# Eight of forty expert steps select their token rows with TensorE instead of gathering them, and one token tile's shared-expert products move later

## The chip, the cores and the metric

The kernel runs on one core of one Trainium2 chip. The metric is the device time of one execution in microseconds (us); the kernel before takes 987.73 us, the median of three runs. All data are f32 unless the text says otherwise.

## What is computed

One decoder layer for 512 tokens of 1024 channels. The first half (a pooling mixer and a windowed attention, gated and projected) is not touched by the change. The second half, cut to what matters:

```python
h2 = rmsnorm(x, g_ffn).reshape(T, D)             # T = 512, D = 1024
idx, wts = route(h2, w_router, router_bias)      # 8 of 64 experts a token, limited to groups
moe = routed_experts(h2, idx, wts, w_exp_gate, w_exp_up, w_exp_down) \
    + swiglu(h2, w_sh_gate, w_sh_up, w_sh_down)  # the shared expert
x = x + moe.reshape(B, S, D)
ple_gate = sigmoid(rmsnorm(x, g_ple) @ w_ple_gate)
x = x + ple_gate * rmsnorm(p @ w_ple_proj, g_ple_post)

def swiglu(x, wg, wu, wd):                       # inner width 256, also for each expert
    return (silu(x @ wg) * (x @ wu)) @ wd
```

Every expert has 3 MB of weights (gate, up and down of 1 MB each), so the 64 of them are the bulk of what the kernel reads.

## The kernel before, in words

**Tiles and order.** The 512 tokens are four tiles of 128. The residual x lies in `xrow` (128 x 4 x 1024) through the whole second half. The residual's rows, normed and multiplied by g_ffn (h2), are also stored in DRAM (`h2_rows`). After routing, the experts are put in an order by their number of tokens: the first four are fixed, the rest descends. They are worked off four at a time (a group). Each expert of the first eight groups has 96 places, each of the last eight has 64. A step is 128 places, so a big group has three steps and a small one two: steps 0 to 23 are big, steps 24 (`SMALL_AT`) to 39 small, and a small step holds exactly two experts.

**One step r** is spread over the engines:

- POOL (`move`, L830) gathers the step's rows of h2 from DRAM by an indirect DMA (L821) into one of three buffers `hg` (in `rows`), three steps ahead, as soon as `rows_T(r)` has read the buffer; and it scatters the weighted results of step r to an accumulator in DRAM (L826). Both take their row numbers from a staging tile (L814, L818), and a small operation (a ticket, L809) goes ahead of each.
- PE: `rows_T` (L2265) transposes the 128 gathered rows in eight pieces into two PSUM banks (L1812, a helper's line). DVE copies the first half out (L1605), ACT the second (L999). `up` (L2277, products at L2300) multiplies by gate and up in four strips of 32 places; ACT and DVE make silu x up (L1004, L1610). `acts_T` (L2309) transposes that, DVE copies it out (L1615), and `down` (L2312, products at L2329) multiplies by the down weights. ACT weighs the result (L1012) for the scatter.
- SP loads the weights into a ring of slots: `load_group` (L602) sends loads of the next group as `in_used` and `down_used` show that up and down have freed a slot (L541, L560).

PE's order within step r is `up(r)`, `acts_T(r-1)`, `rows_T(r+1)`, for early steps the lists of a later group (`lists`), jobs of slot 0, `down(r-1)`, jobs of slot 1. DVE goes through `act_T(r-1)`, `act_rows(r)`, `rows_T(r+1)`, lists, jobs; ACT through `silu(r)`, `rows_hi(r+1)`, jobs, `weigh(r-1)`.

**Jobs.** Work that is not the experts' is hung into the small steps by a table, `JOB_STEP` (L60). Numbers 0 to 5 are the shared expert's first products for token tiles 2 and 3 (`LATE`): two groups of four transposes (`late_T`, L2099) and one set of products (`late_up`, L2110 and L2113) a tile. Numbers 6 and 7 transpose the shared expert's inner activations (`shared_T`), 8 to 15 are its down products, added to the residual by DVE (`shared_down` L2249, `base` L1633), and 16 to 23 project p for the last stage (`ple_proj` L2260). All jobs use PSUM bank 5, so each waits for the reader of the one before. Token tiles 0 and 1 have their shared products (`shared_up`, L2124) earlier, in pieces between the operations of routing and ahead of step 0; SP waits for both (L589) before it loads the fourth expert into the slots of the shared weights. An f32 matrix product in the program appears as two MATMULs and two weight loads in the trace, a transpose as one of each.

**After step 39** the accumulator's rows are read back, summed over the eight experts of a token, and the last gate is computed and applied.

Of the kernel before, what the change touches and what calls it, by code (L numbers as in the profile page):

```python
# [76 lines left out]
def jobs_of(step, slot):  # L77

    return [n for n, at in enumerate(JOB_STEP) if at == step and n % 2 == slot]

# [79 lines left out]
SH_BANK = [7, 3, 5, 5]  # L160
# [26 lines left out]
def build(nc, t, y_dram, h2_dram, out):  # L187
    ctx = ExitStack()
    with ctx:
# [19 lines left out]
        gcol = sb("gcol", [P, KD])  # L209
        sink_in = sb("sink_in", [P, NH])  # L210
# [71 lines left out]
        w_ple = [rows[:, 3, :], flat_actT[:, 3 * D:4 * D]]  # L282
        hgT = [lo[:, k * D:(k + 1) * D].rearrange("p (k n) -> p k n", k=KD) for k in range(2)]
# [205 lines left out]
        def _(sp):  # L489
# [99 lines left out]
            sp.wait_ge(shared_ps, 2)  # L589
# [12 lines left out]
            def load_group(g, late):  # L602
# [100 lines left out]
        def _(pool):  # L703
# [35 lines left out]
            small_load(vecs[V_GFFN:V_GFFN + KD, :], t["g_ffn"].rearrange("o (k n) -> (o k) n", n=P))  # L739
            small_load(sink_in[:, :], t["attn_sinks"].broadcast_to([P, NH]))  # L740
# [89 lines left out]
            def move(r, j, before, first=False, last=False):  # L830


                if not last:
                    pool.wait_ge(hgT_ps, 2 * r + 2)
                    stage_from(r + BUF, j)
                    if not first:
                        pool.wait_ge(ticket_done[0], r)
                    pool.wait_ge(staged, 2 * r + BUF + 1)
# [7 lines left out]
                pool.wait_ge(staged, STEPS + r + 1 if last else 2 * r + BUF + 2)  # L846
# [16 lines left out]
            def o_move(e, n, j):  # L863
                pool.wait_ge(o_over, n + 1)
                pool.wait_ge(ticket_done[0], STEPS - BUF + n)
# [32 lines left out]
        def _(act):  # L898
# [123 lines left out]
            def job(n):  # L1022
                if n in (2, 5):
                    shared_silu_of(LATE[n // 3])
                elif n >= 8 + 2 * NT:
                    ple_square(n - 8 - 2 * NT)
# [6 lines left out]
            shared_silu_of(1)  # L1033
            for r in range(STEPS):
# [3 lines left out]
                if r + 1 < STEPS:  # L1038
                    rows_hi(r + 1, (r + 1) % 2)
# [61 lines left out]
        def _(dve):  # L1101
# [457 lines left out]
            shared_mult(1)  # L1559
# [47 lines left out]

            def act_rows(r, k):
# [34 lines left out]
            for r in range(STEPS):  # L1643
# [15 lines left out]
                for n in jobs_of(r, 0) + jobs_of(r, 1):  # L1659
                    if n < 6 and n % 3 < 2:  # L1660
                        late_T(n // 3, n % 3)
                    elif n < 6:
                        shared_mult(LATE[n // 3])
                    elif n < 8:
                        shared_T(n - 6)
                    elif n < 8 + 2 * NT:
                        base(n - 8)
# [822 lines left out]
```

## Time and profile before

| | |
|---|---|
| median of 3 runs | 987.73 us (987.58 to 988.1) |
| the profiled execution | 983.44 us |
| its span, first to last instruction | 981.6 us |
| mean granted clock of TensorE | 0.991 |
| routing ends, first up product of step 0 | 339.6 us from the span's start |
| big steps, 0 to 23 | 339.6 to 630.5 us |
| small steps, 24 to 39 | 630.5 to 903.8 us |
| moved by DMA | 305.08 MB, of which 33.46 MB by gathers and scatters |

Columns of the profile: an engine's busy time is the time under its instructions; matmuls are pipelined and their ends are modelled, so a busy PE need not be PE at its best. PE is TensorE's matmuls, PEld its weight loads, which run beside them; DVE, ACT, POOL and SP are the vector, scalar, GpSimd and sync engines, and SPq is SP's sequencer, which issues DMAs. L1812 is line 1812 of the kernel. PEclk is the clock granted to TensorE as a part of full speed. What stands behind an arrow in brackets is the idle time of the engine and what ended it.

### The profile page before, as it was taken

The page shows a single profiled execution, that of the slowest core. Times are in us where ns is not written, and L with a number is a line of the kernel's source. Part 1 is how long each engine was busy: PE and PEld are TensorE (multiplying, and loading weights), DVE is VectorE, ACT ScalarE, POOL GpSimd, SP SyncE. Part 2 cuts the span into 40 slices and gives each one's busy share as a digit, 9 for nine tenths or more (in the row PEclk, how much of TensorE's full clock was granted, in tenths as well). Part 3 has the DMA queues.
Part 4 walks back from the last instruction along what each step waited for, and adds up shares of the span by engine and source line. Part 5 has one row for each costly group of instructions (what it writes and reads, how often), then busy time and mean ns, then how long its engine had stood idle before and what let it go on. Part 6 is the DMA issues. An engine that isn't in the chain of part 4 may idle for free.

```text
span 981.6 us, 15774 instructions
## 1 busy us (share of the span) xinstructions
PE 937.8 (96%) x6407; PEld 490.9 (50%) x6407; DVE 364.7 (37%) x787; ACT 163.8 (17%) x306; POOL 229.2 (23%) x344
## 2 busy tenths in 40 slices
PE   9999999999999999999999999999879899898888
PEld 7688888888556533333333333354323233332345
DVE  3765774236436733333333111011101111111887
ACT  2001233210011211111111111111101112111121
POOL 4216913262000212222222222212121211201120
PEclk9999999999999999999999999999989999999999
DMA  9970006422473799999999999999999999999982
GB/s 334 384 246 1 1 1 214 129 86 86 144 297 110 246 385 384 396 420 410 399 423 405 412 414 405 411 422 421 414 421 421 421 419 418 419 402 362 347 313 86
DMA packets 86009, 305.08 MB, mean 311 GB/s; under 512 B 9389, under 2 KB 38097, under 8 KB 61744
## 3 DMA queue, kind: packets, MB, share of 16 engines
q1 hardware_dynamic: 72240, 267.38, 69.4%
q0 software_dynamic: 11920, 33.46, 8.7%
q10 hardware_dynamic: 1776, 3.21, 0.9%
q8 instruction: 52, 0.85, 0.3%
q14 instruction: 21, 0.17, 0.0%
HBM read 279.26 MB, written 33.55 MB: 319 GB/s over the span
## 4 chain that ended last, share of the span: by engine, by line
PE 73%; DMA 21%; SPq 2%; DVE 2%; issue 1%; ACT 0%; ACTq 0%; DVEq 0%
PE ps L2300 22%; DMA ring<-in_w_exp_up 18%; PE ps L1903 13%; PE ps L2329 8%; PE ps L2053 6%; PE ps L2032 5%; PE ps L2447 4%; PE ps L1812 2%; PE ps L1845 2%; DMA ring<-in_w_exp_down 2%; PE ps L2124 1%; PE ps L1855 1%; DMA ring<-accumulator 1%; SPq L555 1%; PE ps L2309 1%; SPq L541 1%
## 5 line engine op out<-in xcount | busy, mean ns | idle before, releaser
L2300 PE MATMUL ps<-ring,gates 128*32 128x512 f32 x2560 | 287.1, 600 | 27.9 <-DMA ring<-in_w_exp_up 27.1
L2300 PEld LDWEIGHTS ps<-ring,gates 128*32 128x32 f32 x2560 | 88.3, 111 | 218.7 <-issue 217.8
L2329 PE MATMUL ps<-ring,poolbuf 128*32 128x512 f32 x1280 | 147.3, 601 | 3.0 <-DMA ring<-in_w_exp_down 2.1
L1615 DVE COPY poolbuf<-ps 128x256 f32<-128x256 f32 x40 | 17.0, 425 | 355.8 <-PE ps L2309 355.8
L809 POOL TENSOR_TENSOR tickets<-cst 128x1 f32<-128x1 f32 x77 | 14.5, 188 | 398.2 <-ACT actT L1012 392.8
L2329 PEld LDWEIGHTS ps<-ring,poolbuf 128*32 128x32 f32 x1280 | 38.3, 110 | 84.6 <-issue 83.0
L1012 ACT ACTIVATE actT<-ps,qT 128x1024 f32<-128x1024 f32 x40 | 44.5, 1113 | 143.9 <-PE ps L2329 143.9
L1004 ACT ACTIVATE poolbuf<-ps 128x256 f32<-128x256 f32 x40 | 15.4, 384 | 279.6 <-PE ps L2300 279.6
L1903 PE MATMUL ps<-xrow,ring 128*128 128x256 f32 x256 | 57.9, 381 | 0.1
L2053 PE MATMUL ps<-ring,gates 128*128 128x512 f32 x128 | 56.4, 594 | 0.0
L1903 PEld LDWEIGHTS ps<-xrow,ring 128*128 128x128 f32 x256 | 48.3, 190 | 8.4 <-issue 1.7
L1903 PE MATMUL ps<-actT,ring 128*128 128x256 f32 x208 | 47.5, 381 | 0.0
L821 POOL DMA_INDIRECT rows<-h_rows,stage x40 | 41.8, 1045 | 21.4 <-issue 19.0
L1812 PE MATMUL ps<-cst,rows 128*128 128x128 f32 x352 | 46.1, 274 | 0.0
L826 POOL DMA_INDIRECT accumulator<-actT,stage x40 | 40.6, 1016 | 22.2 <-issue 22.2
L1812 PEld LDWEIGHTS ps<-cst,rows 128*128 128x128 f32 x352 | 43.0, 190 | 2.0 <-issue 1.8
L2447 PE MATMUL ps<-ring,actT 128*128 128x512 f32 (+1 forms) x112 | 42.9, 535 | 0.0
L1903 PEld LDWEIGHTS ps<-actT,ring 128*128 128x128 f32 x208 | 39.0, 190 | 6.3 <-issue 0.9
L759 POOL TENSOR_TENSOR ring<-ring 128x1024 f32<-128x1024 f32 x12 | 28.3, 2357 | 52.4 <-DMA ring<-in_w_gate 30.2
L2053 PEld LDWEIGHTS ps<-ring,gates 128*128 128x128 f32 x128 | 23.8, 190 | 26.8 <-issue 26.8
L2447 PEld LDWEIGHTS ps<-ring,actT 128*128 128x128 f32 x112 | 21.1, 193 | 18.3 <-issue 17.5
L727 POOL TENSOR_SCALAR st<-st 128x1 f32<-128x1 f32 (+2 forms) x17 | 4.7, 276 | 108.0 <-ACT rows L957 50.0
(306 smaller groups left out, 1086.3 us busy)
## 6 DMA issues: line engine op xcount, KB each, us to landing
ring<-in_w_exp_down SPq DMA_DIRECT2D x64, 1024.0 KB, 17.3
ring<-in_w_exp_gate SPq DMA_DIRECT2D x62, 1024.0 KB, 13.5
ring<-in_w_exp_up SPq DMA_DIRECT2D x62, 1024.0 KB, 16.5
ring<-accumulator SPq DMA_DIRECT2D x10, 1024.0 KB, 13.5
ring<-in_w_gate SPq DMA_DIRECT2D x8, 1024.0 KB, 11.8
accumulator<-ring SPq DMA_DIRECT2D x2, 4096.0 KB, 22.6
ring<-in_w_in SPq DMA_DIRECT2D x5, 1024.0 KB, 10.1
ring<-accumulator SPq DMA_DIRECT2D x10, 512.0 KB, 9.5
```

The source lines that it names most:

```text
L759: nc.gpsimd.tensor_tensor(dst, a, b, ALU.subtract).then_inc(wsum_ready, 1)
L821: pool.indirect_dma_start(hg[j], None, h2_dram, bass.IndirectOffsetOnAxis(ap=stage[:, 0, j, :], axis=0), bounds_check=T - 1, oob_is_err=Fa ...
L826: pool.indirect_dma_start(y_dram, bass.IndirectOffsetOnAxis(ap=stage[:, 1, j, :], axis=0), yrow[j], None, bounds_check=ACC_ROWS - 1, oob_i ...
L1012: nc.scalar.activation(yrow[j], bank(6, 2), ACT.Copy, scale=slot_wr[:, r, 0:1]).then_inc(y_ready, 1)
L1812: last = nc.tensor.transpose(bank(b0 + half)[:, k * width:(k + 1) * width], v[0:width, 4 * half + k, :], ident[0:width, 0:width])
L1845: last = mm(bank(2 * (i % 2)), actT[:, k, i * P:(i + 1) * P], qv[:, k], start=(k == 0), stop=(k == KD - 1))
L1903: last = mm(out[:, f * HALF_T:(f + 1) * HALF_T], w[:, k, f * P:(f + 1) * P], x[:, k, :], start=(k == 0), stop=(k == 3))
L2032: last = mm(bank(2 + c % 4)[:, f * HALF_T:(f + 1) * HALF_T], w[:, k, (2 * p + f) * P:(2 * p + f + 1) * P], x[:, k, :], start=(k == 0), sto ...
L2053: last = mm(bank(half), gates[:, k, i * P:(i + 1) * P], w[:, k], start=(n == 0), stop=(n == KD - 1))
L2300: last = mm(bank(2 + k)[part, :], hgT[k][:, q, part], pair_view(EXPERT_SLOT[js[c]])[:, q], start=(q == 0), stop=(q == KD - 1))
L2329: last = mm(bank(6 + half)[part, :], eactT[r % 2][:, q, part], w[:, q, half * 512:(half + 1) * 512], start=(q == 0), stop=(q == 1))
L2447: last = mm(gate_bank(i, n0)[:, 0:width], xT, unit_view(s, 4)[:, k % 4, n0 % 512:n0 % 512 + width], start=(k == 0), stop=(k == KD - 1))
```

## The change

Steps 28 to 35 (`CHOSEN`) are no longer gathered. Two steps ahead, DVE makes for such a step a matrix `chosen` of 128 tokens x 4 tiles x 128 places: an entry is the token's reciprocal norm where the token holds that place of that expert, and 0 elsewhere (two operations; it lies in the buffer that the gather would have filled). PE multiplies the residual's tiles by it, summed over the four tiles, so that the products come out as the transposed rows that `rows_T` would have made; DVE copies both halves out and multiplies by g_ffn, which is loaded once by POOL in a layout by partition (`gffn_col`). POOL's counts of gathers and tickets skip these steps. ACT's `rows_hi` falls away for them.

`LATE` has token tile 1 as well, so `shared_up(1, ...)` goes from the stretch ahead of step 0, and three jobs come in. The jobs' table gets new places: late tiles in steps 24 to 28, `shared_T` in 29, four `shared_down` each in steps 34 and 35 (two a slot), `ple_proj` in 36 to 39. SP's load of w_sh_down moves from behind step 27's up to behind step 29's.

```diff
-LATE = (2, 3)
+LATE = (1, 2, 3)
+LATE_JOBS = 3 * len(LATE)
-JOB_STEP = [SMALL_AT + n // 2 for n in range(8)] + [SMALL_AT + 6 + n // 2 for n in range(4 * NT)]
+JOB_AT = [(SMALL_AT + n // 2, n % 2) for n in range(LATE_JOBS)] + [(SMALL_AT + 5, n) for n in range(2)] + \
+    [(SMALL_AT + 10 + n // 4, n % 4 // 2) for n in range(2 * NT)] + \
+    [(SMALL_AT + 12 + n // 2, n % 2) for n in range(2 * NT)]
+CHOSEN = range(SMALL_AT + 4, SMALL_AT + 12)
...
+        chosen = [h[:, 0:NT * P].rearrange("p (i n) -> p i n", i=NT) for h in hg]
...
-            sp.wait_ge(shared_ps, 2)
+            sp.wait_ge(shared_ps, 1)
             load_in(3, 3)
...
-                    if step == SMALL_AT + 2:
+                    if step == SMALL_AT + 4:
                         load_shared_down()
...
+            small_load(gffn_col[:, :], t["g_ffn"].rearrange("o (p k) -> (o p) k", k=KD))
...
-                if not last:
+                fetched = gathers(range(min(r + BUF + 1, STEPS)))
+                if not last and r + BUF not in CHOSEN:
                     pool.wait_ge(hgT_ps, 2 * r + 2)
                     stage_from(r + BUF, j)
...
-            shared_silu_of(1)
             for r in range(STEPS):
...
-                if r + 1 < STEPS:
+                if r + 1 < STEPS and r + 1 not in CHOSEN:
                     rows_hi(r + 1, (r + 1) % 2)
...
+            def choose(r):
+                g, s = STEP_OF[r]
+                dve.wait_ge(hgT_ps, 2 * (r - BUF) + 2)
+                at = chosen[r % BUF]
+                e, cap = g * GROUP + pair_of(g, s), cap_of(g)
+                link(nc.vector.tensor_tensor(
+                    at.rearrange("p i (e r) -> p i e r", r=cap),
+                    cst[:, C_IOTA + CAP - cap + 1:C_IOTA + CAP + 1].unsqueeze(1).unsqueeze(1).broadcast_to(
+                        [P, NT, P // cap, cap]),
+                    rank3[:, :, e:e + P // cap].unsqueeze(3).broadcast_to([P, NT, P // cap, cap]), ALU.is_equal))
+                nc.vector.tensor_tensor(at, at, st[:, 1, 0:NT].unsqueeze(2).broadcast_to([P, NT, P]), ALU.mult
+                                        ).then_inc(rows_ready, 1)
+            def chosen_T(r, k):
...
+                for half, done in enumerate((hgT_lo_ready, hgT_hi_ready)):
+                    dve.wait_ge(hgT_ps, 2 * r + half + 1)
+                    nc.vector.tensor_tensor(
+                        hgT[k][:, 4 * half:4 * half + 4, :], bank(half).rearrange("p (k n) -> p k n", k=4),
+                        gffn_col[:, 4 * half:4 * half + 4].unsqueeze(2).broadcast_to([P, 4, P]), ALU.mult
+                    ).then_inc(done, 1)
...
                 act_rows(r, r % 2)
-                if r + 1 < STEPS:
+                if r + 1 in CHOSEN:
+                    chosen_T(r + 1, (r + 1) % 2)
+                elif r + 1 < STEPS:
                     rows_T(r + 1, (r + 1) % 2)
+                if r + 2 in CHOSEN:
+                    choose(r + 2)
...
-            shared_up(1, 0, 2)
...
-            shared_up(1, 2, 4)
...
+            def chosen_T(r):
+                pe.wait_ge(rows_ready, NT + CHOSEN.index(r) + 1)
+                pe.wait_ge(hgT_lo_ready, r)
+                pe.wait_ge(hgT_hi_ready, r)
+                v = xrow.rearrange("p i (q k) -> p i k q", k=KD)
+                for half in range(2):
+                    for k in range(4):
+                        for i in range(NT):
+                            last = mm(bank(half)[:, k * P:(k + 1) * P], v[:, i, 4 * half + k, :],
+                                      chosen[r % BUF][:, i, :], start=(i == 0), stop=(i == NT - 1))
+                    last.then_inc(hgT_ps, 1)
...
             rows_T(0)
-            shared_up(1, 4, 8)
...
-                if r + 1 < STEPS:
+                if r + 1 in CHOSEN:
+                    chosen_T(r + 1)
+                elif r + 1 < STEPS:
                     rows_T(r + 1)
```

## Rows read from the trace of the kernel before

**Rows 1.** The page, part 1: busy time and share of each engine.
```profile
PE 937.8 (96%) x6407; PEld 490.9 (50%) x6407; DVE 364.7 (37%) x787; ACT 163.8 (17%) x306; POOL 229.2 (23%) x344
```

**Rows 2.** The page, part 4: the chain that ended last, by engine.
```profile
PE 73%; DMA 21%; SPq 2%; DVE 2%; issue 1%; ACT 0%; ACTq 0%; DVEq 0%
```

**Rows 3.** Timeline of PE, steps 16 and 17: start, length in us.
```profile
532.27 7.05 PE L2300 MATMUL ps<-ring,gates 128*32 128x512 f32 x64
...
539.59 1.04 PE L1812 MATMUL ps<-cst,rows 128*128 128x128 f32 x8
540.56 3.64 PE L2329 MATMUL ps<-ring,poolbuf 128*32 128x512 f32 x32
544.02 7.05 PE L2300 MATMUL ps<-ring,gates 128*32 128x512 f32 x64
```

**Rows 4.** Windows: steps 24, 28, 29, 30, 33, 39, and steps 28 to 39.
```profile
core 0: us, PE busy (x) PEld busy (x) DVE busy (x) ACT busy (x) POOL busy (x), PEclk, DMA share, GB/s
630.49:645.23 14.74, 12.98 (x115) 5.32 (x116) 2.70 (x5) 2.09 (x3) 3.01 (x7) 1.00 1.01 415
...
696.98:714.46 17.48, 11.96 (x108) 4.14 (x108) 2.04 (x4) 2.84 (x4) 5.39 (x11) 0.96 1.02 421
714.46:731.79 17.33, 14.72 (x106) 4.83 (x107) 1.35 (x3) 2.09 (x3) 0.89 (x4) 0.84 1.01 421
731.79:749.17 17.38, 15.59 (x114) 5.80 (x115) 2.73 (x5) 2.09 (x3) 3.76 (x9) 1.00 1.02 421
784.80:802.16 17.36, 17.30 (x115) 6.27 (x116) 2.07 (x5) 2.09 (x3) 1.10 (x3) 0.90 1.01 417
882.91:903.80 20.89, 17.04 (x137) 5.38 (x129) 1.29 (x4) 2.61 (x3) 2.76 (x6) 0.92 1.00 372
696.98:903.80 206.82, 181.98 (x1364) 65.87 (x1363) 27.90 (x54) 30.77 (x52) 32.41 (x69) 0.97 1.01 413
```

**Rows 5.** Timeline of PE: late products (step 25), router products, warming products and transposes.
```profile
653.46 1.89 PE L2110 MATMUL ps<-gates,mixw 128*128 128x256 f32 x8
...
660.46 3.64 PE L2329 MATMUL ps<-ring,poolbuf 128*32 128x512 f32 x32
...
302.30 1.89 PE L2077 MATMUL ps<-gates,actT 128*128 128x64 f32 x16
304.03 0.39 PE L2063 MATMUL ps<-cst,xrow 128*128 128x128 f32 x2
...
1.04 3.78 PE L1823 MATMUL ps<-kT 128*128 128x128 f32 x16 [1.04 <-DVE kT L1127]
4.97 1.91 PE L1812 MATMUL ps<-cst,xrow 128*128 128x128 f32 x8
```

**Rows 6.** Timeline of DVE, step 30: the addition behind one shared down product.
```profile
741.94 0.69 DVE L1633 TENSOR_TENSOR xrow<-xrow,ps 128x512 f32<-128x512 f32 x1 [1.25 <-PE ps L2249]
```

**Rows 7.** The page, part 3: the queue of the gathers and scatters.
```profile
q0 software_dynamic: 11920, 33.46, 8.7%
```

**Rows 8.** Timeline of PE, ACT, SP and DVE ahead of step 0.
```profile
329.55 1.98 PE L2124 MATMUL ps<-ring,actT 128*128 128x512 f32 x4
...
335.21 1.05 PE L1812 MATMUL ps<-cst,rows 128*128 128x128 f32 x8
336.09 3.60 PE L2124 MATMUL ps<-ring,actT 128*128 128x512 f32 x8
339.62 7.07 PE L2300 MATMUL ps<-ring,gates 128*32 128x512 f32 x64
...
336.34 0.59 ACT L999 ACTIVATE gates<-ps 128x512 f32<-128x512 f32 x1
...
333.85 0.38 SPq L585 DMA_DIRECT2D gates<-in_w_sh_gate  x1
...
344.09 0.46 DVE L1557 TENSOR_SCALAR kT<-rows 128x256 bf16<-128x256 f32 x1
```

**Rows 9.** The page, part 5: up and down products, with their idle time.
```profile
L2300 PE MATMUL ps<-ring,gates 128*32 128x512 f32 x2560 | 287.1, 600 | 27.9 <-DMA ring<-in_w_exp_up 27.1
...
L2329 PE MATMUL ps<-ring,poolbuf 128*32 128x512 f32 x1280 | 147.3, 601 | 3.0 <-DMA ring<-in_w_exp_down 2.1
```

More of the change, by code:

```diff
@@ L77, in jobs_of, with gathers @@
 def jobs_of(step, slot):
-    return [n for n, at in enumerate(JOB_STEP) if at == step and n % 2 == slot]
+    return [n for n, at in enumerate(JOB_AT) if at == (step, slot)]
+def gathers(steps):
+    return sum(1 for r in steps if r not in CHOSEN)
 def cap_of(g):
@@ L158 @@
 N_DENSE = len(DENSE)
-SH_BANK = [7, 3, 5, 5]
+SH_BANK = [7, 5, 5, 5]
 LOGIT_BANK = [4, 6, 4, 6]
@@ L209, in build @@
         gcol = sb("gcol", [P, KD])
+        gffn_col = sb("gffn_col", [P, KD])
         sink_in = sb("sink_in", [P, NH])
@@ L836, in move @@
                     if not first:
-                        pool.wait_ge(ticket_done[0], r)
-                    pool.wait_ge(staged, 2 * r + BUF + 1)
+                        pool.wait_ge(ticket_done[0], fetched - BUF - 1)
+                    pool.wait_ge(staged, r + fetched)
                     ticket(0, ticket_done[0])
@@ L845, in move @@
                     pool.wait_ge(ticket_done[1], r)
-                pool.wait_ge(staged, STEPS + r + 1 if last else 2 * r + BUF + 2)
+                pool.wait_ge(staged, fetched + r + 1)
                 pool.wait_ge(y_ready, r + 1)
@@ L864, in o_move @@
                 pool.wait_ge(o_over, n + 1)
-                pool.wait_ge(ticket_done[0], STEPS - BUF + n)
+                pool.wait_ge(ticket_done[0], gathers(range(BUF, STEPS)) + n)
                 pool.wait_ge(o_list_ready, n + 1)
@@ L1022, in job @@
             def job(n):
-                if n in (2, 5):
+                if n < LATE_JOBS and n % 3 == 2:
                     shared_silu_of(LATE[n // 3])
-                elif n >= 8 + 2 * NT:
-                    ple_square(n - 8 - 2 * NT)
+                elif n >= LATE_JOBS + 2 + 2 * NT:
+                    ple_square(n - LATE_JOBS - 2 - 2 * NT)
             shared_silu_of(0)
@@ L1659, in _ @@
                 for n in jobs_of(r, 0) + jobs_of(r, 1):
-                    if n < 6 and n % 3 < 2:
+                    if n < LATE_JOBS and n % 3 < 2:
                         late_T(n // 3, n % 3)
-                    elif n < 6:
+                    elif n < LATE_JOBS:
                         shared_mult(LATE[n // 3])
[L1664 to L1667, printed above, removed]
+                    elif n < LATE_JOBS + 2:
+                        shared_T(n - LATE_JOBS)
+                    elif n < LATE_JOBS + 2 + 2 * NT:
+                        base(n - LATE_JOBS - 2)
                     else:
-                        ple_gain(n - 8 - 2 * NT)
+                        ple_gain(n - LATE_JOBS - 2 - 2 * NT)
             act_T(STEPS - 1, (STEPS - 1) % 2)
@@ L2268, in rows_T @@
                 j = r % BUF
-                pe.wait_ge(gathered[j], 16 * (r // BUF + 1))
+                pe.wait_ge(gathered[j], 16 * gathers(range(j, r + 1, BUF)))
                 if r:
@@ L2321, in down @@
                 else:
-                    pe.wait_ge(shared_act, 2)
+                    pe.wait_ge(shared_act, 1)
                     pe.wait_ge(tokw_ready, 1)
@@ L2334, in job @@
             def job(n):
-                if n < 6 and n % 3 < 2:
+                if n < LATE_JOBS and n % 3 < 2:
                     late_T(n // 3, n % 3)
-                elif n < 6:
+                elif n < LATE_JOBS:
                     late_up(n // 3)
-                elif n < 8:
-                    shared_T(n - 6)
-                elif n < 8 + 2 * NT:
-                    shared_down(n - 8)
+                elif n < LATE_JOBS + 2:
+                    shared_T(n - LATE_JOBS)
+                elif n < LATE_JOBS + 2 + 2 * NT:
+                    shared_down(n - LATE_JOBS - 2)
                 else:
-                    ple_proj(n - 8 - 2 * NT)
+                    ple_proj(n - LATE_JOBS - 2 - 2 * NT)
             rows_T(0)
-            shared_up(1, 4, 8)
             for r in range(STEPS):
```

7 lines of the change are left out of this document (3 added, 4 removed).

## The prediction

> **What bounds the kernel now.** I read the page first. Its busy line shows PE at 937.8 of 981.6 us [rows 1], which says little by itself, since matmuls are pipelined and a stretch of half clock counts as busy too. The chain of waits comes second: 73% of the span runs over PE and 21% over DMA [rows 2], so there are two kinds of stage. The timeline of a step with 96 places per expert shows the first kind: from one up product (532.27) to the next (544.02) PE has no gap, 11.75 us [rows 3]. There PE is the limit. The table of windows by step shows the second kind, in the steps of 64 places (24 to 39): steps 30 and 33 each take 17.4 us, with the 16 DMA engines full (share 1.01) at 417 to 421 GB/s, while PE is busy 15.59 of 17.38 us in step 30 [rows 4]. So the transfers are the limit there, and PE's margin is what counts. It is small, because jobs already lie in it. From 696.98 to 903.80 PE is busy 181.98 of 206.82 us [rows 4], which leaves 24.84 us idle. A part of the busy time is half clock besides: steps 28 and 29 issue the same work, but PE needs 11.96 us in one and 14.72 us in the other, whose granted clock is 0.84. That step follows a wait of 17.48 - 11.96 = 5.5 us, so the clock fell from 2.4 to 1.2 GHz in the gap and came back during the step.
>
> **Part 1: eight steps are selected by PE.** A gathered step costs PE eight transposes: 540.56 - 539.59 = 0.97 us on the timeline, 0.88 us as the spacing goes (0.110 us each) [rows 3]. A selected step is 2 halves x 4 k x 4 token tiles = 32 f32 products of 128 by 128 by 128. An f32 product is two MATMULs with a weight load each: the late products of one token tile are 16 products, and the timeline has four groups of 8 MATMULs, of which the first stands here [rows 5]. So it is 64 pairs. No row has this shape at full clock, and its price lies between neighbours. With 256 columns a pair takes 7.00 us / 32 = 0.219 us (653.46 to 660.46), which halves to 0.109 if streaming sets it; with 64 columns, where streaming can't, 16 pairs start in 302.30 to 304.03, so 0.108 each, the weight load alone [rows 5]. Both limits meet at 128 columns. The warming products at the very start have the exact shape, at half clock: 16 in 3.78 us, and transposes behind them 8 in 1.91 us. Less the last one's tail both are spaced by about 0.22 us, so a pair costs what a transpose costs, and at full clock a transpose costs 0.110. I take 0.110: 64 x 0.110 = 7.04 us, or 6.16 more than the transposes, and for eight steps **+49.3 us** of PE. Bounds: 0.108 (-1.0 us) and, if load and stream that are equally long disturb each other, 0.13 (+10.2). The Trainium skill, TensorE: Matmul & The Clock Gate, section Back-to-back issue gap, gives about 81 ns for a sustained matmul of 128 columns with its load; by it a selected step would be an estimated 5.2 us and the sum 15 us lower, but the router's 0.108 with half the columns is already above that, so the trace does not agree.
>
> The rest of this part is covered. DVE makes the selection matrix two steps ahead (two operations of 512 elements) and evicts both halves instead of one, some 0.69 us each by the same size in [rows 6], so 2 us more in a step of which DVE now works 2.73 us [rows 4]. The second eviction starts when the last product ends, and down of the step before (3.64 us [rows 3]) lies between that and the next up; without that cover it would be 0.8 us a step. ACT loses an eviction, which frees nothing that is waited for. On POOL eight gathers, eight copies and eight tickets go. Queue q0 moved 33.46 MB in 80 indirect transfers [rows 7], about 0.42 MB each; eight gathers are some 3.3 MB, or 8 us at 420 GB/s. That is worth time only where transfers are the limit, and below they no longer are. POOL's one small load more (0 to 0.5 us, taken as 0: PE's work on other tiles covers it).
>
> **Part 2: token tile 1 moves.** Eight products leave the stretch ahead of step 0 and come back as two groups of four transposes, together 1.0 us by the eight of [rows 3], and the late products, 7.00 us [rows 5]: **+8.0 us** of PE in steps 24 to 28. What the removal gives is read in the stretch from 329.55: L2124 runs there in three pieces, two of 1.9 us (the first stands here) and one of 3.5 [rows 8]. PE waits on other things under them, so not all 7.3 us come back. The rows of step 0 have landed when SP goes on at 333.85 (it waits for just that), so the transposes can start at 333.9 instead of 335.21. ACT's second eviction ended at 336.93, 1.72 us after they started, so up can start at about 335.8, some issue time included, instead of 339.62: **-3.8 us**. DVE's work on the weights, which ended at 344.55, must be done when step 0's up ends near 342.9; its input's products stand behind the first piece of L2124, so it starts earlier too, by up to 1.9 us. Where it starts no earlier, 1.7 go back. SP's wait for the shared products ends earlier, but behind it stand only the fourth expert's loads, which step 2 is the first to need. Bounds: 0 (the clock falls in the new gaps, or the transfers hold the later steps where they were) to -4.
>
> **Part 3: the jobs move.** Products of w_sh_down are now two in a slot, on one bank, in steps 34 and 35. The second of each pair waits for DVE's addition (0.69 us [rows 6]), with nothing between: four stalls of about 0.8, **+3.2 us** (0 to 4). Between the pairs, down covers it. The ple products are the same eight, now in steps 36 to 39. SP's wait for the shared products moves from step 26 to 28, where the products are done a step before, and nothing behind it waits.
>
> **What the waits give back.** With 7.04 in place of 0.88 a job-free step of PE is 11.75 + 6.2 = 17.9 us, and the transfers of such a step without its gather are 17.4 - 1.0 = 16.4 us. So in steps 27 to 35 PE becomes the limit, the loads run ahead, and the last four steps (15.6 us of PE) live on that lead. Of the 24.84 us idle all goes but 0.9, which is down's wait in [rows 9] that is not on a transfer (3.0 - 2.1, ACT's copy ahead of the last down). The half clock goes with the gaps: 14.72 - 11.96, 17.30 - 15.59 and, by its clock of 0.92, 20.89 x 0.08 in the last step, 6.2 us [rows 4]. Together **-30.1 us**. Up waits 27.1 us for its loads in all [rows 9]; less the 23.9 - 2.1 of this stretch, 5.3 us lie earlier (1.76 of them in step 24), before the first selection. They stay in the sum, and may go.
>
> **The sum:** 49.3 + 8.0 + 3.2 - 3.8 - 30.1 = +26.6 us. It is made against the profiled execution (983.44 us, of which the span is 981.6), so 1010.0 there. The median of the runs shown is 987.73, 4.3 us above it, and the forecast is 987.7 + 26.6 = **1014.3 us**.
>
> **Rivals.** (a) *The products fit under the transfers*: faster. The chain's 21% on DMA [rows 2] speaks for it. Its place is steps 27 to 34 and its condition a price: with 30.1 us of cover and 11.2 us taken by parts 2 and 3, each selected step may cost 18.9 / 8 = 2.4 us more than now, so 3.2 us, before the stage grows. At one instruction per product (32 x 0.110 = 3.5 us) the sum is 21.1 + 11.2 - 3.8 - 30.1 = -1.6, and with the 5.3 us of early waits gone as well -6.9: 981 us. Against it stand the two MATMULs per f32 product in [rows 5]. (b) *Load and stream don't overlap*: slower still. A pair is then 0.108 + 0.107 = 0.215 us, a selected step 13.8, the sum +80, 1068 us. A rule speaks for it: the Trainium skill, same page, section Part 3: Packing small matmuls, says that a weight load overlaps matmuls in flight only if its row group differs. Against it are the pairs of 256 columns at 0.219, which have no room for a load of 0.108 outside the stream [rows 5], so by that rule the trace does not agree. (c) *DVE sets the selected steps*: its new work (2 us) and the eviction uncovered on the path, 8 x 1.4 = 11 us more, 1025 us. Down's 3.64 us speak against it. (d) *No gain at the start*: PE idles there under fewer products, the clock falls, and up of step 0 takes 2.8 us longer, as in step 29: 1014.3 + 6.6 = 1021 us. This is inside the range.
>
> **How the numbers follow.** Forecast with (d) 0.86 (0.72 and 0.14), (a) 0.05, (b) 0.03, (c) 0.03, something not seen 0.03. The low end takes the forecast with price 0.108, no pair stalls and the early waits gone (-1.0 - 3.2 - 5.3 leaves 1004.8): 1004. The high end takes price 0.13, or (c): 1026. Left out are (a), (b) and half of the unseen. A measurement of this kernel tells about 0.2% (2 us) from no change. Faster 0.05 is (a) and a little of the unseen; (a) may also end within 0.2%, 0.02; slower 0.93.
>
> **What would show it.** Right: the line of the selecting products in eight groups of 64 MATMULs, each about 7 us; steps 29 to 33 at 17.9 us with no idle time on PE and the DMA share below 1; granted clock 1.00 from step 26 on; up of step 0 near 335.8. Wrong: groups near 3.5 us (then (a)), or near 14 us (then (b)); PE still waiting for the up loads in steps 29 to 36; idle time ahead of up put down to DVE's new eviction (then (c)). If PE stays gap-free and the groups take 7 us, but the time is below 1004, then I have mistaken how much idle time there was.

## The result and the profile after

The changed kernel takes 1079.6 us (median of five runs, 1079.14 to 1082.15), against 987.73 us before: a ratio of 1.0942 [1.0925, 1.0959], so it is slower by 91.9 us. The profiled execution is one of these runs (1079.6 us, span 1077.3, mean granted clock 0.995), so its sums need no shift. The kernel before has its profile from an execution of 983.44 us, 4.3 us under its median, so the spans of the two profiles differ by 95.7 us (1077.3 - 981.6) where the medians differ by 91.9. The forecast was 1014.3 us: the sign is right, the size is not, and the time lies far above the range.

The page of the changed kernel: the busy engines, the queue of the gathers, the chain of waits, and the groups of the up products (L2348, before L2300) and of the selecting products (L2323).

```profile
PE 1049.6 (97%) x6879; PEld 605.5 (56%) x6879; DVE 382.6 (36%) x813; ACT 159.0 (15%) x298; POOL 218.6 (20%) x321
...
q0 software_dynamic: 10800, 29.61, 7.0%
...
PE 89%; DMA 8%; DVE 2%; issue 1%; ACT 0%; SPq 0%; POOL 0%; ACTq 0%; POOLq 0%; DVEq 0%
...
L2348 PE MATMUL ps<-ring,gates 128*32 128x512 f32 x2560 | 285.3, 598 | 8.9 <-DMA ring<-in_w_exp_up 7.3
...
L2323 PE MATMUL ps<-rows,xrow 128*128 128x128 f32 x512 | 123.1, 401 | 0.0
L2323 PEld LDWEIGHTS ps<-rows,xrow 128*128 128x128 f32 x512 | 122.5, 335 | 0.0
```

The chain has gone from 73% PE and 21% DMA [rows 2] to 89% and 8%, and up waits 7.3 us for its loads, not 27.1 [rows 9]. That much was forecast. What was not is the last two rows. The eight selected steps hold 123.1 us of PE, 15.4 each, where the prediction has 7.04. The weight loads of these products take 335 ns each. PE had 111.8 us more to do in all (1049.6 - 937.8), and no idle time stands before the product's line (0.0): it is not a wait, it is work.

The timeline of PE through one selected step (step 30 into 31; start, length in us):

```profile
772.60 7.07 PE L2348 MATMUL ps<-ring,gates 128*32 128x512 f32 x64
...
779.95 15.38 PE L2323 MATMUL ps<-rows,xrow 128*128 128x128 f32 x64
795.26 3.64 PE L2377 MATMUL ps<-ring,poolbuf 128*32 128x512 f32 x32
798.72 7.05 PE L2348 MATMUL ps<-ring,gates 128*32 128x512 f32 x64
```

The 64 pairs go from 779.95 to 795.2, so 15.2 us, 0.238 us each. From up to up the step takes 26.1 us instead of the 17.9 forecast. The windows say the same of the whole stretch: the first of the eight groups, the selected steps with the jobs of steps 34 and 35, and the stretch ahead of step 0.

```profile
core 0: us, PE busy (x) PEld busy (x) DVE busy (x) ACT busy (x) POOL busy (x), PEclk, DMA share, GB/s
692.40:707.60 15.20, 15.20 (x66) 15.20 (x65) 1.44 (x3) 0.28 (x1) 0.00 (x0) 1.00 0.73 291
692.30:952.00 259.70, 256.58 (x1560) 169.20 (x1563) 38.78 (x67) 18.01 (x27) 18.92 (x41) 1.00 0.69 261
...
329.00:340.00 11.00, 8.11 (x61) 4.43 (x64) 8.26 (x26) 3.91 (x6) 4.34 (x5) 0.84 0.67 209
```

In 259.70 us PE is idle for 3.12, its clock is full and the transfers take 0.69 of the engines, where before they took all of them (1.01 to 1.02 in [rows 4]). A group of products shows a third thing: PEld is busy for all of its 15.20 us. The loads are back to back, and the products follow at their pace.

The timeline at the start, at the ups of steps 15 and 25, and in the pairs of shared down products (L2286, before L2249):

```profile
335.41 8.35 PE L2348 MATMUL ps<-ring,gates 128*32 128x512 f32 x64 [0.79 <-ACT gates L1043]
...
345.58 7.07 PE L2348 MATMUL ps<-ring,gates 128*32 128x512 f32 x64 [0.73 <-DVE gates L1616]
...
520.13 7.07 PE L2348 MATMUL ps<-ring,gates 128*32 128x512 f32 x64 [2.50 <-DMA ring<-in_w_exp_up]
...
644.55 8.77 PE L2348 MATMUL ps<-ring,gates 128*32 128x512 f32 x64 [3.10 <-DMA ring<-in_w_exp_up]
...
902.23 1.98 PE L2286 MATMUL ps<-gates 128*128 128x512 f32 x4 [0.78 <-DVE xrow L1668]
```

Step 0 starts 4.2 us earlier than in [rows 8], and step 1's up is 2.9 us ahead of its place before (345.58 against 348.51). A lead of 2.7 us lasts to step 14. Then step 15's up waits 2.50 us for its load and starts at 520.13, just as before, and by step 25 only 0.7 us is left (644.55 against 645.23 before). The pair's stall of 0.78 us stands in the last row.

Windows of the kernel before, big steps 0 to 17 (columns as above):

```profile
340.00:445.00 105.00, 104.27 (x1096) 41.75 (x1092) 39.86 (x137) 16.84 (x26) 21.42 (x46) 1.00 1.00 395
445.00:557.00 112.00, 110.96 (x1090) 41.70 (x1082) 31.95 (x123) 19.75 (x28) 25.42 (x54) 1.00 1.01 411
```

PE is busy nearly throughout there, but the transfers take all of the DMA engines as well (1.00 and 1.01), and in the changed kernel the same two stretches show 1.00 and 1.00.

### The profile page after: what moved, and what is told of

Its sections match the earlier page's. It is cut to its first block, busy times and chain, and to the rows that moved or that the text cites. A ratio compares the mean times of both kernels' runs of the same rounds, so it can differ in the third digit from the quotient of the medians.

```text
span 1077.3 us, 16691 instructions
## 1 busy us (share of the span) xinstructions
PE 1049.6 (97%) x6879; PEld 605.5 (56%) x6879; DVE 382.6 (36%) x813; ACT 159.0 (15%) x298; POOL 218.6 (20%) x321
## 3 DMA queue, kind: packets, MB, share of 16 engines
q0 software_dynamic: 10800, 29.61, 7.0%
## 4 chain that ended last, share of the span: by engine, by line
PE 89%; DMA 8%; DVE 2%; issue 1%; ACT 0%; SPq 0%; POOL 0%; ACTq 0%; POOLq 0%; DVEq 0%
PE ps L2348 24%; PE ps L1942 11%; PE ps L2323 11%; PE ps L2377 11%; DMA ring<-in_w_exp_up 7%; PE ps L2092 5%; PE ps L2071 4%; PE ps L2496 4%; PE ps L1851 2%; PE ps L1884 2%; PE ps L2286 1%; PE ps L2297 1%; PE ps L1894 1%; PE ps L2357 1%; PE ps L2149 1%; PE ps L2152 1%
## 5 line engine op out<-in xcount | busy, mean ns | idle before, releaser
L2348 PE MATMUL ps<-ring,gates 128*32 128x512 f32 x2560 | 285.3, 598 | 8.9 <-DMA ring<-in_w_exp_up 7.3
L2348 PEld LDWEIGHTS ps<-ring,gates 128*32 128x32 f32 x2560 | 84.5, 111 | 199.5 <-issue 197.6
L2323 PE MATMUL ps<-rows,xrow 128*128 128x128 f32 x512 | 123.1, 401 | 0.0
L2323 PEld LDWEIGHTS ps<-rows,xrow 128*128 128x128 f32 x512 | 122.5, 335 | 0.0
L1638 DVE TENSOR_TENSOR gates<-ps,gffn_col 128x512 f32<-128x512 f32 x16 | 11.1, 692 | 110.2 <-PE ps L2323 110.2
L1851 PE MATMUL ps<-cst,rows 128*128 128x128 f32 x288 | 38.0, 275 | 1.3 <-DMA rows<-h_rows,stage 1.3
L833 POOL DMA_INDIRECT rows<-h_rows,stage x32 | 34.3, 1072 | 17.7 <-issue 15.3
## 6 DMA issues: line engine op xcount, KB each, us to landing
accumulator<-ring SPq DMA_DIRECT2D x2, 4096.0 KB, 22.6
```

What stands on the lines that cost most here:

```text
L833: pool.indirect_dma_start(hg[j], None, h2_dram, bass.IndirectOffsetOnAxis(ap=stage[:, 0, j, :], axis=0), bounds_check=T - 1, oob_is_err=Fa ...
L1851: last = nc.tensor.transpose(bank(b0 + half)[:, k * width:(k + 1) * width], v[0:width, 4 * half + k, :], ident[0:width, 0:width])
L2323: last = mm(bank(half)[:, k * P:(k + 1) * P], v[:, i, 4 * half + k, :], chosen[r % BUF][:, i, :], start=(i == 0), stop=(i == NT - 1))
L2348: last = mm(bank(2 + k)[part, :], hgT[k][:, q, part], pair_view(EXPERT_SLOT[js[c]])[:, q], start=(q == 0), stop=(q == KD - 1))
```

## The experiments

Each set of runs had the kernel before on the same chip: 986.43 us for the first four, 987.43 for the next four, 984.07 and 985.47 for the last two. The kernels in which every step has a form of its own ran once each, so what is compared there are groups within one execution. In all of the experiments the question is where 0.238 us a pair comes from, and whether the rest of the sum was right.

**Packed weight columns (e1_packed).** One line of the changed kernel: which channels of the residual make up the 128 columns of a weight tile.

```diff
-                v = xrow.rearrange("p i (q k) -> p i k q", k=KD)
+                v = xrow.rearrange("p i (k q) -> p i k q", k=KD)
```

> The changed kernel, but PE reads each weight tile of the selecting products as 128 neighbouring channels of the residual instead of every eighth one. It leaves out the channel order that the expert weights need; instructions, shapes and sizes stay. Theory A (the weight load is slow because its 128 columns lie 32 bytes apart): a pair falls from 0.238 to 0.110 us, a selecting group from 15.2 to about 7.0 us, the time to about 1017 us (1005 to 1022): 987.7 - 0.7 + 8.0 + 3.1 + 49.3 - 30.1. Theory B (at 128 columns of stream an f32 weight load does not overlap the stream, whatever its layout): groups stay at 13.8 to 15.2 us and the time at 1068 to 1080 us.

It took 1016.92 us, a ratio of 1.0304 [1.0275, 1.0334]. Its groups of instructions:

```profile
L2323 PE MATMUL ps<-rows,xrow 128*128 128x128 f32 x512 | 58.5, 275 | 0.0
L2323 PEld LDWEIGHTS ps<-rows,xrow 128*128 128x128 f32 x512 | 57.9, 192 | 0.0
```

The same 512 pairs fall from 123.1 to 58.5 us of PE and their loads from 335 to 192 ns. A selected step, from up to up, takes 18.0 us (787.36 to 805.38), where the prediction has 17.9. So the stride of the weight columns (eight places, 32 bytes from one column to the next) carries 62.7 (1079.6 - 1016.92) of the 65.3 us by which the time lies above the forecast.

**Eight forms of the product (e2_forms).** Each of the eight selected steps has a form of its own.

```diff
-                v = xrow.rearrange("p i (q k) -> p i k q", k=KD)
+                step, width = {28: (1, 128), 29: (2, 128), 30: (4, 128), 31: (8, 128), 32: (8, 256), 33: (1, 256),
+                               34: (16, 128), 35: (8, 512)}[r]
...
+                            v = x_flat[:, at:at + P * step].rearrange("p (q k) -> p k q", k=step)
```

> The disputed price by itself: each of the eight selected steps issues another form of the selecting product. Steps 28 to 31: 128 columns of stream, weights with a stride of 1, 2, 4 and 8 elements; step 34: stride 16. Step 32: stride 8 with 256 columns (16 products), step 33: stride 1 with 256 columns, step 35: stride 8 with 512 columns (8 products). It leaves out the right selection of these steps. Theory A (stride of the weight load): a pair takes 0.110 us at stride 1 and grows with the stride to 0.238 at 8; at stride 8 the load still hides under a longer stream, so 256 columns take 0.238 a pair (load-bound) and 512 columns 0.43 to 0.44 (stream-bound); stride 1 with 256 columns 0.216. Theory B (no overlap): 0.215 to 0.238 at every stride with 128 columns, about 0.33 to 0.45 with 256 columns and 0.55 to 0.67 with 512.

The timeline of PE, the forms in the order of the steps (a length holds the last product's tail of 0.1 to 0.2 us; the figures below go from the group's start to that of the next instruction):

```profile
693.67 7.31 PE L2327 MATMUL ps<-rows,xrow 128*128 128x128 f32 x64
...
712.85 7.70 PE L2327 MATMUL ps<-rows,xrow 128*128 128x128 f32 x64
...
738.17 15.09 PE L2327 MATMUL ps<-rows,xrow 128*128 128x128 f32 x64
...
765.12 15.38 PE L2327 MATMUL ps<-rows,xrow 128*128 128x128 f32 x64
...
791.22 7.89 PE L2327 MATMUL ps<-rows,xrow 128*128 128x256 f32 x32
...
809.82 7.07 PE L2327 MATMUL ps<-rows,xrow 128*128 128x256 f32 x32
...
827.60 14.12 PE L2327 MATMUL ps<-rows,xrow 128*128 128x128 f32 x64
...
852.43 7.14 PE L2327 MATMUL ps<-rows,xrow 128*128 128x512 f32 x16
```

With 128 streamed columns a pair costs 0.112 us at stride 1, 0.118 at 2, 0.233 at 4, 0.239 at 8 and 0.220 at 16. The price doubles between 2 and 4 and does not rise further. With stride 8 it costs 0.244 under 256 streamed columns and 0.436 under 512. At 256 the load is a little over the packed pair's 0.219, and at 512 it has gone under the stream. So load and stream do overlap, and the longer of the two sets the pace.

**The parts apart: tile 1 alone (e3_tile1) and selection alone (e4_select).**

```diff
-CHOSEN = range(SMALL_AT + 4, SMALL_AT + 12)
+CHOSEN = range(0)
```

> The other part alone: token tile 1 late and the new table of jobs, no selected step (all forty are gathered). Theory of the sum: the 8.0 us of late products go into the idle time and the half clock of steps 28 and 29 (5.5 + 2.8 us), the transfers stay the limit, and the time is 982 to 992 us, the upper part because four jobs a step in 34 and 35 and two in 38 and 39 lie outside the idle time. Rival (tile 1 and the pairs' stalls are on the path in full): 987.7 - 0.7 + 8.0 + 3.1 = 998 us.

It took 992.13 us, 1.0057 [1.0037, 1.0077], at the upper end of what was expected. The loss is at the end. A timeline of PE's up products shows waits as before up to 803.06, and then the steps with four shared down products each, which take 22.6 and 21.1 us:

```profile
803.06 8.62 PE L2348 MATMUL ps<-ring,gates 128*32 128x512 f32 x64 [3.71 <-DMA ring<-in_w_exp_up]
825.67 7.07 PE L2348 MATMUL ps<-ring,gates 128*32 128x512 f32 x64
846.74 7.07 PE L2348 MATMUL ps<-ring,gates 128*32 128x512 f32 x64
```

The jobs of two steps are bunched in one, above the 17.4 us that the transfers allow, while other steps go on waiting.

The second kernel goes the other way: token tile 1 is done early, as before, and the eight steps are selected.

```diff
-LATE = (1, 2, 3)
+LATE = (2, 3)
...
+            shared_up(1, 0, 2)
...
+            shared_up(1, 2, 4)
...
+            shared_up(1, 4, 8)
```

> The selection alone: eight selected steps and the new table, but token tile 1 has its shared products ahead of step 0 as before. If the terms of the sum add (tile 1 costs 8.0 us and gives back 0.7), 1072 us. Rival (tile 1's products were covered by idle time of steps 24 to 28): 1079 us, the changed kernel's own time.

It took 1072.14 us, 1.0874 [1.0841, 1.0907], so selection and table alone cost 85.7 us over the kernel before beside it (986.43). It is 7.5 us under the changed kernel, where tile 1 has 8.0 - 0.7 = 7.3 in the sum: the terms add.

**Tile 1 with its jobs spread (e5_spread), and a start that keeps its loads (e6_early).**

```diff
-    [(SMALL_AT + 10 + n // 4, n % 4 // 2) for n in range(2 * NT)] + \
-    [(SMALL_AT + 12 + n // 2, n % 2) for n in range(2 * NT)]
-CHOSEN = range(SMALL_AT + 4, SMALL_AT + 12)
+    [(SMALL_AT + 7 + n // 2, n % 2) for n in range(2 * NT)] + \
+    [(SMALL_AT + 11 + n // 2, n % 2) for n in range(2 * NT)]
+CHOSEN = range(0)
```

> Token tile 1 late and no selected step, as in e3_tile1, but the later jobs lie one in a slot as before: shared_T in step 29, shared_down in 31 to 34, ple_proj in 35 to 38. Theory (what e3_tile1 lost against before came from four jobs a step in 34 and 35 and from jobs in the last step; tile 1 itself is covered): the loss goes, 984 to 988 us. Rival (tile 1's late products cost time by themselves): still 990 to 994 us.

986.59 us, 0.9991 [0.9974, 1.0008]: no measurable difference. So the 5.7 us of the kernel with tile 1 alone (992.13 - 986.43) came from the bunching: from step 34's up to step 39's it takes 90.3 us (803.06 to 893.31), the kernel with spread jobs 84.6 (802.21 to 886.76). The 8.0 us of added work lie under the transfers. The next kernel adds one move to it, SP's loads of the fourth expert ahead of its wait for the first gather:

```diff
+            sp.wait_ge(shared_ps, 1)
+            load_in(3, 3)
...
-            sp.wait_ge(shared_ps, 1)
-            load_in(3, 3)
```

> e5_spread, with the fourth expert's gate and up loads sent as soon as token tile 0's shared products are done, ahead of SP's wait for the first gather. Theory (from step 18 on the transfers set the pace, so what counts is when their stream starts): 2 MB, 5 us at 420 GB/s, are moved into a stretch where the DMA engines are half idle, and 2 to 5 us are won against e5_spread: 980 to 985 us. Rival (the start is lost again, since the loads slow the first gather or the slots come free no earlier): as e5_spread, within 1 us.

988.0 us, 1.0012 [0.9992, 1.0033]: the gain did not come. SP's timeline shows the two loads issued at 328.29 and 328.66, not at 339.02 and 339.55 as in the run before. PE's shows what they cost. First the kernel with spread jobs, where the first transposes start at 333.77:

```profile
333.77 1.46 PE L1851 MATMUL ps<-cst,rows 128*128 128x128 f32 x8 [1.17 <-DMA rows<-h_rows,stage]
335.96 9.69 PE L2348 MATMUL ps<-ring,gates 128*32 128x512 f32 x64 [0.73 <-issue]
```

Then the one with early loads:

```profile
336.85 1.97 PE L1851 MATMUL ps<-cst,rows 128*128 128x128 f32 x8 [4.63 <-DMA rows<-h_rows,stage]
339.56 9.00 PE L2348 MATMUL ps<-ring,gates 128*32 128x512 f32 x64 [0.73 <-issue]
```

The wait for the gathered rows has grown from 1.17 to 4.63 us. From 325 us to the landing of these rows the queues moved 264 GB/s instead of 101: the loads went beside the gather that step 0 waits for, and its rows came 3.1 us later, although POOL issued it no later (328.92 against 329.29). Step 0's up is back at 339.56, where it was before (339.62).

**Packed weights with the weights' rows reordered (e7_packed_right), and two selected steps (e8_two).** The packed tile has another order of channels; here the gate and up weights of the selected groups are loaded in that order too, in pieces of 1 KB.

```diff
+                    w = t[("w_exp_gate", "w_exp_up")[n]][0].rearrange("e (k p) f -> e p k f", p=P)
...
-                        gffn_col[:, 4 * half:4 * half + 4].unsqueeze(2).broadcast_to([P, 4, P]), ALU.mult
+                        vecT[:, V_GFFN + 4 * half:V_GFFN + 4 * half + 4].unsqueeze(2).broadcast_to([P, 4, P]), ALU.mult
...
-                v = xrow.rearrange("p i (q k) -> p i k q", k=KD)
+                v = xrow.rearrange("p i (k q) -> p i k q", k=KD)
```

> The changed kernel with all eight selected steps, but right with neighbouring channels: gate and up weights of the four selected groups are loaded with channel k x 128 + p on partition p (pieces of 1 KB in place of 8 KB), so the selecting products read packed weight tiles, and g_ffn comes from the table that the late products use. Theory A (only the stride was mispriced): groups of 7.1 to 7.3 us and 1014 to 1020 us, as e1_packed. Rival (1 KB pieces slow the loads, and transfers become the limit again): PE waits for up loads in steps 30 to 37 and over 1025 us.

1016.11 us, 1.028 [1.0252, 1.0309], as in the first experiment. The packed order gives 63.5 us back (1079.6 - 1016.11), and the change as a whole, with its eight selected steps, the late tile and the stalls, still costs 28.7 us against the kernel before. The rival falls: PE's ups wait 6.3 us for loads in all, the last time at step 25. The small pieces have a price all the same, for from 711 to 830 us the transfers take 1.02 of the engines at 353 GB/s, against 0.93 at 358 in the first experiment. The last of this set selects two steps only, packed, with early loads and spread jobs.

```diff
-CHOSEN = range(SMALL_AT + 4, SMALL_AT + 12)
+CHOSEN = range(SMALL_AT + 6, SMALL_AT + 8)
```

> e6_early with two selected steps (30 and 31, packed weight tiles as in e7_packed_right), where no job lies; shared_down in 32 to 35, ple_proj in 36 to 39. Theory: with a price of 7.2 us two selected steps take 2 x 6.3 us of PE where some 2 x 1.8 to 2 x 5 are idle, and take 2 x 1 us from the transfers, so nothing or up to 3 us is lost against e6_early, and jobs in the last step cost 2 to 4 more: 983 to 989 us. Rival (transfers are the whole limit, PE's work is covered): 2 us less than e6_early.

991.75 us, 1.0044 [1.0026, 1.0062], 3.75 us above the kernel with early loads and no selection, and outside what was expected. Two selected steps add 2 x 6.3 = 12.6 us of PE. The up products' waits for loads fall from 24.7 to 17.9 us and their busy time, which holds the half clock, from 287.5 to 284.5, so 9.8 us come back. That leaves 2.8, and the two profiled spans differ by 2.9 (987.9 - 985.0). It is not all the selection's, for the later jobs lie one step further on as well, and two that project p fall in the last step: step 39's up starts 1.6 us later (890.98 against 889.41), and the other 1.3 come after that. So two packed selections did not pay, but what they cost by themselves was not measured. No version ran measurably faster than the kernel before.

**Is it the load, the product or the operand? (e9_loads).** The strided transposes of the kernel before had cost 0.110 us each [rows 3]. Again each selected step has a form: T is a transpose, cols64 has 64 streamed columns, rows64 has 64 weight columns, and swap exchanges the operands.

```diff
+                form, step = {28: ("T", 8), 29: ("T", 1), 30: ("cols64", 8), 31: ("cols64", 1),
+                              32: ("rows64", 8), 33: ("mm", 3), 34: ("swap", 8), 35: ("T", 16)}[r]
```

> Why did the strided transposes of the kernel before cost 0.110 us each, when a pair of the strided product costs 0.238? In the eight selected steps the product is replaced by one form each, 64 MATMULs of f32, the results are not the reference's: step 28 transposes of the residual with stride 8; 29 transposes with stride 1; 30 products with weights of stride 8 and 64 streamed columns; 31 the same with stride 1; 32 products with 64 weight columns of stride 8 and 128 streamed columns; 33 products with stride 3; 34 the two operands exchanged, so that stride 8 is on the streamed side and the weights are packed; 35 transposes with stride 16. Theory A (the slow strided load belongs to the weights of a product, whatever streams; a transpose's load is another and fits under its stream): 28, 29 and 35 take 7.0 us each (0.110 x 64), with a mean load near 189 ns in 28 and 140 in 29 as in the kernel before; 30 takes 15.2 (0.238 x 64), 31 6.9 (0.108 x 64); 32, if the load goes by the weight columns that are read, 0.119 x 64 = 7.6; 33 lies between 7.5 and 15.2; 34 takes 7.2. Rival B (any strided load is slow, and the transposes only looked cheap because they come in eights, so that the first loads run ahead): 28 and 35 take 14 to 15 us, 29 takes 7.0. Rival C (stride costs on either operand): 34 takes 15 us.

The timeline of PE, in the order of the steps 28, 30, 31, 33 and 34:

```profile
692.43 7.36 PE L2330 MATMUL ps<-cst,xrow 128*128 128x128 f32 x64
...
736.42 15.38 PE L2332 MATMUL ps<-rows,xrow 128*128 128x64 f32 x64
...
765.10 7.26 PE L2332 MATMUL ps<-rows,xrow 128*128 128x64 f32 x64
...
801.85 11.30 PE L2338 MATMUL ps<-rows,xrow 128*128 128x128 f32 x64
...
823.87 15.09 PE L2336 MATMUL ps<-xrow,rows 128*128 128x128 f32 x64
```

64 transposes in a row cost 0.112 us each at stride 8, 0.109 at stride 1 and 0.113 at 16, so rival B falls: transposes are spared, and not because they come in eights. With 64 streamed columns a pair costs 0.237 at stride 8 and 0.112 at stride 1: the load alone sets it. With 64 weight columns it is 0.124. Stride 3 costs 0.175. But theory A is wrong of the exchanged operands: 0.235 us, so a strided streamed side is as slow as strided weights, and rival C holds there.

**What about a stride is slow? (e10_lines).** The streamed side alone is patterned, and one step has stride 8 on both sides.

```diff
+                form, step, run, off = {28: ("s", 8, 2, 0), 29: ("s", 8, 2, 3), 30: ("s", 16, 4, 0), 31: ("s", 2, 1, 0),
+                                        32: ("s", 3, 1, 0), 33: ("ws", 8, 1, 0), 34: ("s", 4, 1, 0), 35: ("s", 1, 1, 0)}[r]
```

> What about a strided operand is slow? The groups so far are 64 f32 MATMULs a step, 128 columns: stride 1, 2, 3, 4, 8 take 0.112, 0.118, 0.175, 0.233, 0.238 us each, and with the stride on the streamed side 0.234. Here each selected step has one pattern of the streamed operand, with packed weights (the results are not the reference's): step 28 pairs of neighbours at every 8th place, a pair inside one aligned line of 16 bytes; step 29 the same pairs shifted by three places, so that a pair straddles two lines; step 30 four neighbours (one whole line) at every 16th place; step 31 stride 2; step 32 stride 3; step 33 stride 8 on both operands; step 34 stride 4; step 35 stride 1. Theory A (the time goes by the lines of 16 bytes that the 128 columns touch in turn, 1.83 ns each, with a floor of 0.112 us; the Trainium skill, Advanced Engine Details and Errata, section Memory Cachelines, describes such lines): 28 has 64 lines, 7.5 us for the group; 29 has 128, 15.2; 30 has 32, 7.1; 31 7.5; 32 11.2; 34 15.0; 35 7.1. Rival B (it goes by the mean distance between columns, which is four places in 28, 29 and 30): the three are the same, 15.0 us. Rival C (it goes by the number of separate runs, wherever they lie): 28 and 29 are the same, 7.5 us. For 33: 15.2 us if the two operands are read beside each other, 30 if one after the other.

The timeline of PE, steps 28, 29, 30 and 33:

```profile
694.29 7.56 PE L2331 MATMUL ps<-xrow,rows 128*128 128x128 f32 x64
...
713.72 14.67 PE L2331 MATMUL ps<-xrow,rows 128*128 128x128 f32 x64
...
746.01 7.31 PE L2331 MATMUL ps<-xrow,rows 128*128 128x128 f32 x64
...
805.28 15.53 PE L2331 MATMUL ps<-rows,xrow 128*128 128x128 f32 x64
```

Pairs of neighbours inside a line of 16 bytes take 7.40 us, the same pairs shifted so that each straddles two lines take 14.49, and whole lines 7.15. The three have the same mean distance, so rival B falls, and the first two have the same number of runs, so rival C falls. Stride 2, 3, 4 and 1 took 7.35, 11.18, 14.60 and 7.14 us. The price goes by the lines touched, about 1.83 ns each (0.234 us / 128), and below 0.112 us a pair it doesn't show. This was shown on the streamed side. Of the weights only plain strides were tried; 1, 2, 3, 4 and 8 follow the same count of lines, and 16, at 0.220 us, lies 6% under it. With both operands strided the group takes 15.47 us: they are read beside each other.

## Why the prediction was wrong

**The price of a pair is the step that failed.** The prediction says "I take 0.110" and bounds it by 0.108 and 0.13; measured is 0.238. The term +49.3 becomes 8 x (15.22 - 0.88) = +114.7, 65.4 us more. It reached its price by two bridges, and each lacked one half of the case. The warming products have the shape of a selecting product, but their operands are packed (a whole stretch of 128 neighbours of `kT`). The transposes of [rows 3] have the stride, but they are no products, and transposes are spared. No row of the kernel before is a strided product, and the text took two rows that agree for two that bear on it. The bound of 0.13 was drawn from load and stream disturbing each other, so the range had no room for another cause.

The trace of before did hold a sign. One view of it that the prediction did not use compares weight loads tile by tile (their durations in ns: least, median, most): L1812 transposes with stride 8, L2063 with neighbouring columns.

```profile
L1812 PEld LDWEIGHTS ps<-cst,rows x352: 186/189/203, 11.4 to 879.1; 128*128 128x128 f32 x176
...
L2063 PEld LDWEIGHTS ps<-cst,xrow x32: 138/140/196, 280.3 to 318.9; 128*128 128x128 f32 x32
```

The same tile of 128 x 128 takes 189 ns to load with stride 8 and 140 without. A transpose takes about 0.110 us either way (0.112 with stride 8 and 0.109 without in e9_loads), so the sum of before never paid for it.

**Rival (b)** gave 1068 us, the nearest number, with a chance of 0.03, but its mechanism is refuted. The loads do overlap the stream: stride 8 under 512 columns costs 0.436 us a pair, which is twice the 0.219 of a packed pair of 256 columns and leaves nothing for a load of 0.238. The rule that the prediction weighed there, from the Trainium skill (TensorE: Matmul & The Clock Gate, section Part 3: Packing small matmuls), that a weight load overlaps matmuls in flight only if its row group differs, does not hold in these runs either. That the number came near is luck.

**The other terms** came near, but for the start:

| term | predicted | measured |
|---|---|---|
| part 1, eight selected steps on PE | +49.3 | +114.7 |
| part 2, products of tile 1 come back | +8.0 | +8.0 (late products 7.0, as in [rows 5]) |
| part 2, the start | -3.8 | -0.7 (by step 25) |
| part 3, four stalls | +3.2 | +3.1 (4 x 0.78) |
| idle time and half clock given back | -30.1 | -28.5 (by difference) |
| after the last down | not in the sum | -0.9 |
| sum | +26.6 | +95.7 (spans: 1077.3 - 981.6) |

Two rows need a word. The -28.5 was not measured by itself, so that the sum closes is no proof of it. From step 25's up to the end of the last down the kernel before takes 258.6 us (645.23 to 903.79) and the changed one 355.8 (644.55 to 1000.37); of these 97.3 us more, parts 1 to 3 make +125.8, and the rest is what came back. PE's idle time in this stretch falls from 24.84 to 4.96 us, of which 3.12 are the new stalls; that alone is 23.0 us. The half clock goes but for step 25's up (8.77 us instead of 7.07).

The start came as forecast, step 0's up at 335.41 against 335.8, and was lost in both of the ways that its bound of 0 names. Up of step 0 took 8.35 us instead of 7.07, with a granted clock of 0.84 from 329 to 340 us (part of it at 1.2 instead of 2.4 GHz; 1.00 before), and step 15's up waited for its load. Here the prediction's reading of the big steps fell short: it calls PE the limit there, but the transfers are full too, so a PE that starts earlier only comes to its loads earlier. So rival (d) was partly right.

With packed tiles the forecast's own price nearly holds (58.5 us of PE for eight groups, 7.3 each, against 7.04). Its sum with the lost start is 26.6 + 3.1 = +29.7 us, and the first experiment measured 1016.92 - 986.43 = +30.5. Rival (c) falls: DVE's second eviction comes in the shadow of down, as the part on covered work says. The timeline of DVE shows it at 795.37; it ends at 796.06, 2.7 us before up at 798.72:

```profile
795.37 0.69 DVE L1638 TENSOR_TENSOR gates<-ps,gffn_col 128x512 f32<-128x512 f32 x1 [6.93 <-PE ps L2323]
```

Rival (a) could pay 2.4 us a step, and a selected step costs 14.3, or 6.3 packed. Queue q0 moved 29.61 MB, 3.85 less than in [rows 7], where 3.3 was estimated; the transfers had room by then (0.69 of the engines), and the bytes were worth nothing.

## What to carry to other kernels

A price may be borrowed from another row only if the operation, the shape and the access pattern are all the same; where two rows each share a part, the case that has both parts is still unmeasured, and its range must say so. For f32 products on TensorE, lay out both operands so that neighbouring columns are neighbours in memory, or at least two to an aligned line of 16 bytes, and move an awkward order to where it is cheap (here loading the weights in 1 KB pieces gave 63.5 us back). And when an engine has slack, ask how much per step: by the prediction's sum PE could take 2.4 us a selected step, and even the packed selection needs 6.3.

## What the runs showed of the hardware

An f32 MATMUL of 128 columns with its weight load goes at 0.112 us where both operands are packed, at 0.115 to 0.118 where one has stride 2, 0.175 at stride 3, and 0.22 to 0.24 at strides 4, 8 and 16. It makes little difference which of the two operands is strided (0.239 and 0.235 at stride 8), and both together cost no more than one (0.242). The controls with shifted pairs, made on the streamed side, put it down to aligned lines of 16 bytes.

The Trainium skill, Advanced Engine Details and Errata, section Memory Cachelines, says that SBUF has lines of 16 bytes and that at least two hits on a line are needed for full speed. The runs agree: two hits cost 0.118, one hit 0.233. This rule spoke against the change, and the prediction passed it over. The Trainium skill, SBUF — State Buffer, section Door 1: The DMA port swizzle, adds that four f32 places may be strided for free. Here stride 3 costs 0.175 and stride 4 the full 0.233, so on that the measurement differs.

What stays open is why transposes are spared. 64 of them with stride 8 go at 0.112 us each, though their loads touch a line per column as the products' do. No run here tells what a transpose does otherwise.
